# Values ahead of keys, and single waits in place of three barriers, around the prompt attention of a one-core decoder step

## The reference

```python
z, xbc, dt_raw, q, k, v, qm, gates = _split_cols(xn @ lw["w_in"], IN_SPLITS)
...
q = _partial_rope(q.reshape(b, l, ATT_HEADS, ATT_HEAD_DIM), pos)
k = _partial_rope(k.reshape(b, l, KV_HEADS, ATT_HEAD_DIM), pos)
v = v.reshape(b, l, KV_HEADS, ATT_HEAD_DIM)
y_att = attend(q, k, v).reshape(b, l, ATT_WIDTH)
...
merged = (gs[:, :, 0] * (y_ssd @ lw["w_ssd_out"]) + gs[:, :, 1] * (y_att @ lw["w_attn_out"])
          + gs[:, :, 2] * (y_mem @ lw["w_mem_out"]))
```

## Time and profile before

| | |
|---|---|
| Median of 3 runs | 1859.08 us (1852.27 to 1859.51) |
| Profiled execution: time, span | 1856.02 us, 1854.3 us |
| PE busy, share of the span | 1773.0 us, 96% |
| DVE, ACT, POOL busy | 917.1, 606.0, 959.1 us |
| Mean granted clock of TensorE | 0.977 |
| HBM traffic | 106 GB/s over the span |

### The profile page before, as it was taken

How to read it: one execution, slowest core, us unless ns; L and a number is a source line. 1 busy time by engine, 2 the same in 40 slices (tenths; PEclk the granted TensorE clock), 3 DMA queues, 4 the chain that set the end, 5 groups by cost and what they waited for, 6 DMA issues and landing times.

```text
span 1854.3 us, 35896 instructions
## 1 busy us (share of the span) xinstructions
PE 1773.0 (96%) x13998; PEld 1636.0 (88%) x13998; DVE 917.1 (49%) x1537; ACT 606.0 (33%) x1639; POOL 959.1 (52%) x1091
## 2 busy tenths in 40 slices
PE   7999999999999998998998999999998999999987
PEld 7889888999889998785776998779998999999987
DVE  4866677641774322655665632212225661562453
ACT  3454445523454200455443102321013430331231
POOL 3644444455444465320453634226666886886773
PEclk9999999999999999998999999999998999999998
DMA  3213222323132223111796355633221222222222
GB/s 147 69 57 106 95 68 84 106 58 127 47 106 95 92 80 113 38 55 46 264 306 204 140 183 183 220 121 95 80 80 57 80 86 86 80 80 91 80 74 100
DMA packets 53478, 198.50 MB, mean 107 GB/s; under 512 B 6353, under 2 KB 7378, under 8 KB 49618
## 3 DMA queue, kind: packets, MB, share of 16 engines
q1 hardware_dynamic: 41330, 133.13, 23.1%
q10 hardware_dynamic: 7200, 47.52, 6.9%
q0 software_dynamic: 4800, 15.73, 2.5%
HBM read 180.43 MB, written 15.92 MB: 106 GB/s over the span
## 4 chain that ended last, share of the span: by engine, by line
PE 82%; DVE 6%; ACT 4%; DMA 4%; issue 3%; POOL 1%; SPq 0%; POOLq 0%; DVEq 0%; ACTq 0%
PE dps L221 63%; DMA pages<-kv_pages_dram 2%; DVE cout L816 1%; DMA w_raw<-wstream_dram 1%; PE psLE L1543 1%; PE psY L1290 1%; PE psY L552 1%; PE psY L283 1%; ACT cs_rhs L611 1%; PE psY L488 1%; PE psLE L1987 1%; PE psLE L1949 1%; PE psA L1280 1%; PE psY L1566 1%; ACT cout L659 1%
## 5 line engine op out<-in xcount | busy, mean ns | idle before, releaser
L2416 POOL TENSOR_TENSOR w_lo<-w_raw,w_hi 128x256 fp32r<-128x256 f32 x804 | 685.0, 882 | 16.8
L2412 POOL TENSOR_SCALAR w_hi<-w_raw 128x1024 fp32r<-128x1024 f32 x201 | 215.4, 1072 | 706.3 <-PE dps L221 687.4
L221 PE MATMUL dps<-xn_hi,w_hi 128*128 128x288 f32 x2192 | 486.9, 304 | 14.6 <-DVE xn_lo L306 5.1
L221 PE MATMUL dps<-xn_hi,w_lo 128*128 128x288 f32 x2192 | 474.6, 298 | 0.0
L221 PE MATMUL dps<-xn_lo,w_hi 128*128 128x288 f32 x2192 | 474.3, 298 | 0.0
L221 PEld LDWEIGHTS dps<-xn_hi,w_hi 128*128 128x128 f32 x2192 | 360.3, 192 | 44.3 <-issue 35.8
L221 PEld LDWEIGHTS dps<-xn_lo,w_hi 128*128 128x128 f32 x2192 | 358.8, 192 | 0.0
L221 PEld LDWEIGHTS dps<-xn_hi,w_lo 128*128 128x128 f32 x2192 | 358.2, 191 | 0.0
L221 PE MATMUL dps<-y_hi,w_hi 128*128 128x288 f32 x864 | 187.1, 298 | 5.4 <-POOL w_lo L2416 5.4
L221 PE MATMUL dps<-y_hi,w_lo 128*128 128x288 f32 x864 | 186.0, 297 | 0.0
L221 PE MATMUL dps<-y_lo,w_hi 128*128 128x288 f32 x864 | 186.0, 297 | 0.0
(11 more groups left out here) (371 smaller groups left out, 2621.7 us busy)
## 6 DMA issues: line engine op xcount, KB each, us to landing
w_raw<-wstream_dram SPq DMA_DIRECT2D x217, 512.0 KB, 3.5
pages<-kv_pages_dram SPq DMA_DIRECT2D x68, 256.0 KB, 3.8
pages<-kv_pages_dram POOLq DMA_DIRECT2D x60, 256.0 KB, 4.0
st_in<-state_t_dram ACTq DMA_DIRECT2D x8, 1024.0 KB, 4.8
ssm_s_dram<-st_in ACTq DMA_DIRECT2D x8, 1024.0 KB, 5.6
kc<-mem_kt_dram ACTq DMA_DIRECT2D x4, 2048.0 KB, 8.5
vc<-mem_v_dram ACTq DMA_DIRECT2D x3, 2048.0 KB, 7.8
h_res<-x_t_dram ACTq DMA_DIRECT2D x1, 2304.0 KB, 9.1
```

The lines of the kernel that those rows point to most:

```text
L221: mm = pe.matmul(dps[:, par, b, 0:cw], w, a[:, k, c0:c0 + cw], start=(k == 0 and j == 0), stop=(k == nk - 1 and j == 2))
L2412: pool.tensor_scalar(w_hi[:, par, :], w_raw[:, par, :], 1.0, 1.0, ALU.mult, ALU.mult).then_inc(w_hi_done, 1)
L2416: ins = pool.tensor_tensor(w_lo[:, par, at], w_raw[:, par, at], w_hi[:, par, at].bitcast(F32), ALU.subtract)
```

## The change

Four things are edited. The two value tiles come ahead of the two key tiles in the weight stream and in the three programs of the key and value stage; the value transposes and `v_new` now stand between the key tiles. The three barriers before, between and after the key and value stage and the attention are gone; in their places stand waits for the semaphores that the next work needs. For the first pair, the second half of the projection of pair 1 stands ahead of its scores. And around the last pair's turns, PE does two quarters of the first gate tile, the own scores and the scores of page step 0, with DVE's part of these ahead of its last `y_lo`. The tile `own` changes its place in memory, so that it doesn't lie over `v_tok`.

```diff
         def pe_kv(pe):
...
+            for u in range(3):
+                pe_dense(pe, slot(n_kv, u), xn_hi, xn_lo)
             for u in range(2):
-                pe_dense(pe, slot(n_kv, u), xn_hi, xn_lo)
+                par, k0 = slot(n_kv, u)
+                pe.wait_ge(dense_free[par], k0 + 1)
             pe.wait_ge(cst_b_in, 16)
-            rotated(0)
-            pe_dense(pe, slot(n_kv, 2), xn_hi, xn_lo)
-            rotated(1)
-            pe_dense(pe, slot(n_kv, 3), xn_hi, xn_lo)
-            par, k0 = slot(n_kv, 3)
-            pe.wait_ge(dense_free[par], k0 + 1)
             for c in range(CH):
...
             mm.then_inc(vt_full, 1)
+            rotated(0)
+            pe_dense(pe, slot(n_kv, 3), xn_hi, xn_lo)
             pe.wait_ge(vt_copied, 1)
...
             mm.then_inc(vt_full, 1)
+            rotated(1)
         def act_kv(act):
...
+            act.wait_ge(merged_done, KT)
+            act.sem_inc(sam_start, 1)
             act.dma_start(cst_b[:], io["cst"][:, CST_A:CST_W]).then_inc(cst_b_in, 16)
...
             act.dma_start(io["kv_t"][:, 2:4, :], vs[:]).then_inc(kv_out, 16)
+            key(0)
+            key_high(0)
+            key(1)
+            key_high(1)
+            act.wait_ge(kv_out, 16)
             act.dma_start(io["kv_t"][:, 0:2, :], ks[:]).then_inc(kv_out, 16)
-            act.wait_ge(kv_out, 32)
         def dve_kv(dve):
...
+            dve.wait_ge(merged_done, KT)
             dve.memset(qbd[:], 0.0)
...
+            rope(dve, link, ks[:, 0, :], 1, 1)
+            key_low(0)
             dve.wait_ge(vt_full, 2)
             dve.tensor_copy(v_new[:], psA[:, 0:256]).then_inc(vt_copied, 1)
+            rope(dve, link, ks[:, 1, :], 2, 2)
+            key_low(1)
+            dve.wait_ge(vt_copied, 2)
+            dve.wait_ge(kv_out, 16)
         def pe_q(pe):
...
                 if not last:
                     pe_project(pe, t + 1, 0)
+                if t == 0:
+                    pe_project(pe, 1, 1)
                 pe_scores_q(pe, t, 0)
                 if t:
                     pe_turns(pe, t - 1, 2)
-                if not last:
+                if t and not last:
                     pe_project(pe, t + 1, 1)
...
+            pe.wait_ge(s_exp, (KT - 2) * CH + CH - 1)
+            pe_gate1(pe, 0, 0)
             pe_turns(pe, KT - 1, 2)
+            pe_own_scores(pe)
+            pe_gate1(pe, 0, 1)
             pe_turns(pe, KT - 1, 3)
+            pe.wait_ge(s_exp, KT * CH)
+            pe_scores(pe, 0)
             pe_products_q(pe, KT - 1)
         def dve_q(dve):
...
             dve_norm_q(dve, link, KT - 1, 3)
+            dve_own(dve, link)
+            dve_scores(dve, 0)
             dve_y_q(dve, KT - 1)
-            dve.wait_ge(ylo_ready, KT)
-            dve.wait_ge(qbd_done, KT)
-        own, pt_own, own_out = sa("own", [P, NB, TS]), sa("pt_own", [P, CH, P]), sa("own_out", [P, 2, NB // 2 * 64])
+        pt_own, own_out, own = sa("pt_own", [P, CH, P]), sa("own_out", [P, 2, NB // 2 * 64]), sa("own", [P, NB, TS])
...
         def pe_own_scores(pe):
+            pe.wait_ge(s_exp, (KT - 1) * CH + CH - 1)
+            pe.wait_ge(qbd_done, KT)
         def pe_s(pe):
-            pe_own_scores(pe)
             for n in range(STEPS_S + 2):
                 b, c = divmod(n, CHUNKS)
-                if n < STEPS_S:
+                if 0 < n < STEPS_S:
                     pe_scores(pe, n)
...
-                if b < NB - 1:
+                if n >= 2 and b < NB - 1:
                     pe_gate1(pe, b, c)
...
+                if n == 2:
+                    pe.wait_ge(ylo_ready, KT)
                 if n >= 2:
                     pe_values(pe, n - 2)
         def act_s(act):
             act.sem_inc(sam_start, 1)
+            act.wait_ge(kv_out, 32)
             act.wait_ge(own_ready, 1)
...
-            stage_end(pe, 0)
             pe_kv(pe)
-            stage_end(pe, 0)
             pe_q(pe)
-            stage_end(pe, 0)
             pe_s(pe)
...
-    for column in (k_at, k_at + P, v_at, v_at + P):
+    for column in (v_at, v_at + P, k_at, k_at + P):
```

More of the change, by code:

```diff
@@ L1144, in rotated @@
             def rotated(j):
-                par, k0 = slot(n_kv, j)
+                par, k0 = slot(n_kv, 2 + j)
                 pe.wait_ge(dense_free[par], k0 + 1)
                 pe_rot(pe, raw, c_("rot"), rot_full)
+            for u in range(3):
+                pe_dense(pe, slot(n_kv, u), xn_hi, xn_lo)
             for u in range(2):
-                pe_dense(pe, slot(n_kv, u), xn_hi, xn_lo)
+                par, k0 = slot(n_kv, u)
+                pe.wait_ge(dense_free[par], k0 + 1)
             pe.wait_ge(cst_b_in, 16)
-            rotated(0)
-            pe_dense(pe, slot(n_kv, 2), xn_hi, xn_lo)
-            rotated(1)
-            pe_dense(pe, slot(n_kv, 3), xn_hi, xn_lo)
-            par, k0 = slot(n_kv, 3)
-            pe.wait_ge(dense_free[par], k0 + 1)
             for c in range(CH):
@@ L1168, in pe_kv, with key @@
             mm.then_inc(vt_full, 1)
+            rotated(1)
         def act_kv(act):
+            def key(j):
+                par, k0 = slot(n_kv, 2 + j)
+                act.wait_ge(dense_full[par], from_one(k0 + 1))
+                if j:
+                    act.wait_ge(rope_done, 1)
+                act.activation(two(raw[:]), dps[:, par, :, 0:HALF], ACT.Copy).then_inc(dense_free[par], 1)
             def key_high(j):
@@ L1183, in act_kv @@
                 act.wait_ge(dense_full[par], from_one(k0 + 1))
[L1184 to L1191, removed]
+                act.activation(two(vs[:, u, :]), dps[:, par, :, 0:HALF], ACT.Copy).then_inc(dense_free[par], 1)
+            for u in range(2):
                 par, k0 = slot(n_kv, u)
@@ L1194, in act_kv, with key_low @@
             act.dma_start(io["kv_t"][:, 2:4, :], vs[:]).then_inc(kv_out, 16)
+            key(0)
[3 more added lines that the diff above has]
+            act.wait_ge(kv_out, 16)
             act.dma_start(io["kv_t"][:, 0:2, :], ks[:]).then_inc(kv_out, 16)
-            act.wait_ge(kv_out, 32)
         def dve_kv(dve):
             link = chains["dve"]
+            def key_low(j):
+                dve.wait_ge(khi_ready, j + 1)
+                dve.tensor_tensor(k_lo[:, j, :], ks[:, j, 0:SEQ], k_hi[:, j, :].bitcast(F32), ALU.subtract).then_inc(klo_ready, 1)
+            dve.wait_ge(merged_done, KT)
             dve.memset(qbd[:], 0.0)
@@ L1203, in dve_kv @@
             dve.tensor_copy(causal_r[:], c_("causal")).then_inc(masks_ready, 1)
[L1204 to L1208, removed]
             dve.wait_ge(vt_full, 1)
@@ L1744, in dve_s @@
             link = chains["dve"]
-            dve_own(dve, link)
             for n in range(STEPS_S + 2):
                 b, c = divmod(n, CHUNKS)
-                if n < STEPS_S:
+                if 0 < n < STEPS_S:
                     dve_scores(dve, n)
@@ L2498, in _ @@
             act_states_out(act)
-            stage_end(act, 1)
-            act.sem_inc(sam_start, 1)
             act_kv(act)
-            stage_end(act, 1)
             act_q(act)
-            stage_end(act, 1)
             act_s(act)
@@ L2523, in _ @@
             merge0.dve(dve)
-            stage_end(dve, 2)
             dve_kv(dve)
-            stage_end(dve, 2)
             dve_q(dve)
-            stage_end(dve, 2)
             dve_s(dve)
```

## The result

The changed kernel took 1845.29 us (median of 7 runs, 1841.65 to 1851.89) against 1859.51 us (7 runs, 1852.27 to 1863.17): ratio 0.9933, 95% interval 0.9911 to 0.9955. A second comparison of the same two kernels gave 1847.35 us (7 runs) against 1857.46 us (15 runs): 0.9958, 0.9940 to 0.9977. By their means the two comparisons give 12.4 and 8.8 us. Over both, the means are 1847.0 and 1857.3 us, a difference of 10.3 us (interval worked out from the spread of the runs: 8.0 to 12.6). The forecast was 1847 us, 9.8 us less than before.

A forecast was written before the change was run, and what follows sets the result against it. PE was taken as the bound, carrying 82% of the chain, so its idle and half-clock time count. Terms 8.7 + 0.8 + 0.3 = 9.8 us, from 1856.0 or 1856.7 us, gave 1847 us; range 1839 to 1854.

The forecast's parts named there:

- Barriers out, values first: Key and value stage: 5.5 us of PE waits and 3.4 of half clock go, 0.2 charged; 8.7 taken, bounds 7 to 9.5.
- GpSimd did not become the pace: Rival, value stage: GpSimd's weight splits come late, removed waits return as waits for weights; 1852 us, chance 0.06.
- The 0.2 for the second key's rotation: Key tiles: PE reaches the second key's rotation close behind that key's eviction, mostly covered by `v_new` products; 0.2 us charged.
- Second half tile of pair 1: First pair: the 1.5 us wait for `q_lo` goes, some waits come back; net 0.8 us, bounds 0 and 1.5.
- The returned waits: First pair, without the half tile's cover: 0.4 us of PE wait comes back, another 0.3 before the fourth score block.
- The last pair and the first page: Passage to the pages: signal 2.0 us sooner, less 1.7 for half clock; net 0.3 us, bounds -2.4 and 5.9.
- 2.0 us sooner: Last pair: ACT raises `sam_start` at 879.0 instead of 881.0, so page step 3 comes at 891.3, not 893.3.
- The sum to the end of `y_hi`, 8.7 us: Last pair at full clock: turns, own scores, gate part, page scores, products and `y_hi` from 870.34 sum to 8.7 us.
- Page 3 did not come early: Rival: the 3.94 us of issue is not GpSimd's first transfer's; page 3 at 887.2, 15.4 us in all, 1841; chance 0.18.
- The tail gave back: Rival: stall before page 3 costs two half-clock stretches; part -2.4 us, 7.1 in all, 1850 us; chance 0.15.
- the slower case: Rival: page 3 stall leaves PE at 1.2 GHz; five steps make it slower by over 0.5%, six give 1870; chance 0.04.
- 0.6 of 0.57: Odds of a gain beyond 9.3 us (0.5%): 0.6 of the main forecast's spread, whose chance is 0.57; given as 0.36.

The follow-up runs named there:

- the version with the later order: Changed kernel with own scores, page step 0 and second gate quarter moved behind the last pair's products: 1843.34 us (6 runs) against the changed kernel's 1847.35 us.

## Why the prediction was right

**Barriers out, values first.** Forecast 8.7 us, measured 8.9 (9.0 between the second executions). The terms were 5.5 us of waits and 3.4 us of half clock, less 0.2. Two pieces are confirmed by runs that undo them: the first barrier is 3.9 us (the 2.2 and 1.7 of the working), the order of the tiles 2.0 (the 1.4 and 0.7). What is left, 8.9 - 5.9 = 3.0 us, fits the second barrier (1.2 and 1.7); no run puts that one back alone. Its half clock is in the second profile of the kernel before too, where PE starts again at 735.97 and 735 to 740 us have 0.66: 5.0 x 0.34 = 1.7 us. GpSimd did not become the pace: PE never waits for `w_lo` there, and the windows from 696 to 702 are full. The 0.2 for the second key's rotation was not needed: PE shows no wait there.

**Second half tile of pair 1.** Forecast 0.8 net of 1.5; measured 0.7, and 0.8 by the run that undoes it. The returned waits were sized at 0.4 and 0.3 us, and the trace has 0.7, 0.4 and 0.2.

**The last pair and the first page.** Net forecast 0.3 us; measured 1.3 and 0.8 us between first and second executions. That this part gained anything is not shown, since the old tail itself took 27.5, 26.8 and 24.2 us in three executions. Behind the signal the mechanism was as described: GpSimd's issue and the transfer paid again (4.18 and 4.04 us), a stall of 5.7 and 5.0 us where some 5 were forecast (the working's own numbers, 891.3 - 878.4 less 4.0 and 3, give 5.9), and 1.6 and 2.1 us lost to the half clock behind it (6.23 and 6.66 us from step 3 to step 4, 4.61 before) where 1.7 was charged. The term that was mis-sized is "2.0 us sooner": the signal came 3.0 us sooner after the third turn (GpSimd released at 881.31 in the kernel before, 11.0 us after the turn, and 8.0 us after it now). GpSimd's release stands in the chain of two runs as follows, first the kernel before, then the run with the key and value stage alone:

```profile
881.31 0.54 POOLq L1470
875.97 0.54 POOLq L1478
```

In that second run the same old tail, barrier included, released GpSimd 7.4 us after the third turn (868.59) at full clock. So the signal that comes sooner is the half clock behind the third turn that is gone, and not the overlap. The working did count on the full clock there, and it came in all eleven executions with a gate quarter ahead of the third turn, while the old tail, with PE idle for 2.3 us before that turn, had it in one execution of three. Why it kept the clock in that one, no run shows. That the measured 1.3 and 0.8 us lie near the forecast 0.3 is in part luck. The sum to the end of `y_hi`, 8.7 us, was right (872.10 + 0.60 - 864.27 = 8.4). What was wrong is that ACT would raise `sam_start` when `y_hi` ends: GpSimd's next instruction starts at 872.22, 0.1 us after `y_hi` starts, and in the chains of seven more runs it is 0.1 us too. ACT's timeline shows the overlap (start us, us, instruction):

```profile
872.10 0.60 ACT L1368 ACTIVATE y_hi<-psY 128x512 fp32r<-128x512 f32 x1 [2.52 <-PE psY L1298]
872.59 0.62 ACT L1684 ACTIVATE own<-own 128x512 f32<-128x512 f32 x1
```

In the kernel before a barrier stood between `y_hi` and the signal, so its trace could not show it.

**What was not forecast.** Between the sixth pair and the last pair's third turn the changed kernel took 1.1 and 1.3 us more. Most of that stretch is unedited, and it differs between executions of one kernel: the version with the later order, which is the changed kernel up to there, took 19.9 us in one execution, as the kernel before did in both, and 21.3 in another. In the changed kernel 0.55 and 0.50 were granted from 850 to 856, behind a wait of 2.1 us for `q_lo` that both kernels have. After step 4 the changed kernel took 2.4 and 2.6 us less. Together that is 1.2 to 1.3 us less, and with the 0.5 to 1.0 us more that the tail gave, the sum of the trace became 11.8 to 12.1 us instead of 9.8. The run times gave 10.3 us, nearer to the forecast than the traces, and that too is in part luck.

**The rivals.** Page 3 did not come early: the 4 us do belong to GpSimd's first load. The tail gave back 1.6 and 2.1 us by the half clock, where 1.7 was charged and 3.4 feared. Set against the old tail at full clock it did lose, 26.3 and 26.0 us against 24.2, which is close to the 2.4 us of that rival, by another way. The half clock behind page step 3 ended within a step (step 4's scores take 1.01 us), so the slower case, PE at 1.2 GHz for several steps, did not occur. Two numbers of the working are a little off in themselves: 0.6 of 0.57 is 0.34 and not 0.36, and five slow steps make 9.2 us, not over 9.3.

## What to carry to other kernels

Each of the two barriers in front of a busy TensorE cost its gap here (2.2 and 1.2 us) and about 1.7 us of half clock behind it, so price both, from the windows right after the gap. A stretch at half clock that only some executions have can pass for the gain of an edit: profile the kernel before more than once, too. Work that can run at any time belongs behind the instruction that raises a signal, into the time in which the signalled engine starts up, not ahead of it: that order took 22.7 and 22.1 us here between the last pair's third turn and page step 4, some 4 us less than the one of the change. An early transfer is worth what the next ones can follow: counted from the third turn, step 3 came 4.5 us sooner by SP, and in that run the steps behind it took more than that back.

## What the hardware showed that was not expected

GpSimd's first page load had 2.4 to 4.2 us of issue ahead of it (2.40, 3.15, 3.31, 3.40, 3.57, 3.60, 3.94, 3.94, 4.05 and 4.18 us in ten executions), and its next load, in the runs where that one did not have to wait for a buffer, had pieces of 0.5 us only. The Trainium skill, GPSIMD Engine Reference, "Instruction dispatch", gives some 6 us for the first call of newly loaded code; the traces agree that it is a cost of the first one only, and the measured size is the smaller one. That code loading is the cause, no run here shows.

After a wait PE did not always fall to the half clock. Behind 5.7 us, 5.0 us and 3.5 us (page step 3) the clock was near 0.5, and behind 2.2 us (first barrier) it was 0.50 to 0.67; behind 1.7 us (page step 3 with the later order) and 1.4 us (keys first) it was 1.00; behind 1.6 us for `q_lo` it was 1.00 in one run and 0.69 in another.
